# An mLSTM output norm's inverse root: from ScalarE's square root and VectorE's reciprocal to one power on POOL

## The reference, cut to what matters

```python
h = num / jnp.maximum(jnp.abs(den), jnp.exp(-m_t))[..., None]
...
def rmsnorm(x, g):
    xf = x.astype(jnp.float32)
    y = xf * lax.rsqrt(jnp.mean(xf * xf, axis=-1, keepdims=True) + EPS)
    return (y * g).astype(x.dtype)
...
hm = rmsnorm(hm, mlstm_norm_g).astype(x.dtype)
y_b = jax.nn.sigmoid(o) * hm.reshape(B, L, MLSTM_WIDTH)
```

## Time and profile before

| | us |
|---|---|
| median of 3 runs | 1203.65 |
| lowest, highest | 1203.19, 1204.58 |
| the profiled execution, its own time | 1207.14 |
| its span, first to last instruction | 1205.3 |
| TensorE busy in it | 1153.6 |
| VectorE, ScalarE, POOL busy | 704.6, 428.2, 305.3 |

### The profile page before, as it was taken

One profiled execution on the slowest core, in us unless ns is written; L12 is line 12 of the kernel. 1 busy time (PEld: TensorE's weight loads), 2 busy tenths in 40 slices (PEclk: granted clock), 3 DMA queues, 4 the chain that ended last, 5 costly groups with the idle time before them and its releaser, 6 DMA issues.

```text
span 1205.3 us, 19527 instructions
## 1 busy us (share of the span) xinstructions
PE 1153.6 (96%) x7381; PEld 1104.5 (92%) x7381; DVE 704.6 (58%) x1253; ACT 428.2 (36%) x716; POOL 305.3 (25%) x263
## 2 busy tenths in 40 slices
PE   4899999989989999999999999999999999999997
PEld 1698888888978999899999999999999999999996
DVE  5561355577875434777755655655655745656646
ACT  5552354545445343641331320421411311412431
POOL 0441101110525267762120120210210210210352
PEclk9699999999988999999999999999999999999998
DMA  8813434656333822111120121121120211111104
GB/s 307 305 62 110 106 108 137 209 173 197 115 107 106 264 71 72 52 54 36 51 72 23 49 70 36 38 68 34 52 70 17 66 56 32 55 52 36 35 1 141
DMA packets 61702, 109.87 MB, mean 91 GB/s; under 512 B 6434, under 2 KB 30278, under 8 KB 61254
## 3 DMA queue, kind: packets, MB, share of 16 engines
q1 hardware_dynamic: 51430, 84.88, 21.7%
q10 hardware_dynamic: 10208, 24.12, 6.4%
HBM read 96.81 MB, written 12.18 MB: 90 GB/s over the span
## 4 chain that ended last, share of the span: by engine, by line
PE 65%; DVE 2%; ACT 2%; issue 1%; POOL 1%; POOLq 0%; ACTq 0%; DVEq 0%
PE D L2296 13%; PE D L2298 13%; PE D L2297 13%; PE X L2298 5%; PE X L2296 5%; PE X L2297 5%; PE D L2112 3%; PE D L2114 3%; PE D L2113 3%; POOL H_lo L975 0%; DVE X L1556 0%; DVE B L1542 0%; DVE FU L1871 0%; ACT Y_hi L1268 0%; DVE FU L1684 0%
## 5 line engine op out<-in xcount | busy, mean ns | idle before, releaser
L975 POOL TENSOR_TENSOR Y_lo<-FU,Y_hi 128x344 fp32r<-128x344 f32 (+2 forms) x120 | 123.2, 1031 | 560.5 <-ACT Y_hi L1115 554.2
L1831 DVE SCALAR_TENSOR_TENSOR X<-D,MOD,X 128x344 f32<-128x344 f32 (+1 forms) x216 | 123.8, 573 | 136.3 <-PE D L2298 113.8
L2296 PE MATMUL D<-Y_hi,W_hi 128*128 128x344 f32 x576 | 185.2, 322 | 0.0
L2298 PE MATMUL D<-Y_hi,W_lo 128*128 128x344 f32 x576 | 184.1, 320 | 0.0
L2297 PE MATMUL D<-Y_lo,W_hi 128*128 128x344 f32 x576 | 184.1, 320 | 0.0
L2112 PE MATMUL D<-H_hi,W_hi 128*128 128x344 f32 x472 | 160.2, 339 | 3.7 <-POOL H_lo L975 3.1
L2113 PE MATMUL D<-H_lo,W_hi 128*128 128x344 f32 x472 | 153.5, 325 | 0.0
L2114 PE MATMUL D<-H_hi,W_lo 128*128 128x344 f32 x472 | 153.2, 325 | 0.0
L2296 PEld LDWEIGHTS D<-Y_hi,W_hi 128*128 128x128 f32 x576 | 108.5, 188 | 1.2 <-issue 0.9
L970 POOL TENSOR_TENSOR W_lo<-RAWW,W_hi 128x1024 fp32r<-128x1024 f32 x25 | 61.6, 2462 | 186.1 <-ACT W_hi L1110 185.7
L2298 PEld LDWEIGHTS D<-Y_hi,W_lo 128*128 128x128 f32 x576 | 108.5, 188 | 0.0
(11 more groups left out here) (358 smaller groups left out, 2670.8 us busy)
## 6 DMA issues: line engine op xcount, KB each, us to landing
RAWW<-in_W SPq DMA_DIRECT2D x76, 512.0 KB, 3.6
RAWW<-in_WADA ACTq DMA_DIRECT2D x28, 512.0 KB, 4.2
RAWW<-in_WADA SPq DMA_DIRECT2D x20, 512.0 KB, 8.0
RAWW<-in_W ACTq DMA_DIRECT2D x18, 512.0 KB, 4.2
X0T<-in_x SPq DMA_DIRECT2D x3, 1376.0 KB, 12.7
out_y<-OUTN SPq DMA_DIRECT2D x24, 172.0 KB
X<-in_x SPq DMA_DIRECT2D x8, 344.0 KB, 4.6
NM<-nm_d SPq DMA_DIRECT2D x8, 256.0 KB, 5.9
```

Source lines behind the costliest of these rows:

```text
L975: nc.gpsimd.tensor_tensor(lo_v, fu_v, hi_v.bitcast(F32), ALU.subtract).then_inc(lo_ready, 1)
L1831: tell(V.scalar_tensor_tensor(out=tile(X, m_x, a, a + w), in0=DB[bank][:, 0:w], scalar=tile(MOD, m_g, 0, 1), in1=tile(X, m_x, a, a + w), o ...
L2296: T.matmul(out, w_h, hi(kt), start=(kt == 0), stop=False)
L2298: one = T.matmul(out, w_l, hi(kt), start=False, stop=(kt == n - 1))
```

## The change

ScalarE's root in `HN:c` goes. VectorE adds 96 times EPS to the sum of squares in an instruction of its own (row 6 to row 4) and then raises `z_ready`. POOL, in its turn for `HN:c`, waits for `z_ready` and raises row 4 to the power in row 7, which VectorE sets to -0.5 once, in chunk 0. In `HM:c` the reciprocal goes, and the product becomes one of three factors, with the constant sqrt(96).

```diff
@@ POOL @@
+                elif k == "HN":
+                    pool.wait_ge(z_ready, s[1] + 1)
+                    nc.gpsimd.tensor_tensor(SM4[:, 5, :], SM4[:, 4, :], SM4[:, 7, :], ALU.pow).then_inc(z_root, 1)
@@ ScalarE @@
-                elif k == "HN":
-                    act.wait_ge(z_ready, s[1] + 1)
-                    nc.scalar.activation(SM4[:, 5, :], SM4[:, 4, :], ACT.Sqrt, bias=EPT[:], scale=1.0 / HD).then_inc(z_root, 1)
@@ VectorE @@
-                    tell(V.tensor_reduce(SM4[:, 4, :], T1[:, :, 0:HD], AX_X, ALU.add), z_ready, c + 1)
+                    link(V.tensor_reduce(SM4[:, 6, :], T1[:, :, 0:HD], AX_X, ALU.add))
+                    if c == 0:
+                        link(V.memset(SM4[:, 7, :], -0.5))
+                    tell(V.tensor_scalar(SM4[:, 4, :], SM4[:, 6, :], HD * EPS, None, ALU.add), z_ready, c + 1)
...
                     dve.wait_ge(z_root, c + 1)
-                    link(V.reciprocal(SM4[:, 6, :], SM4[:, 5, :]))
-                    tell(V.tensor_tensor(HM[c % 4][:], HM[c % 4][:], wide(SM4[:, 6, :], HD), ALU.mult), hm_ready, c + 1)
+                    tell(V.scalar_tensor_tensor(out=HM[c % 4][:], in0=HM[c % 4][:], scalar=math.sqrt(HD), in1=wide(SM4[:, 5, :], HD),
+                                                op0=ALU.mult, op1=ALU.mult), hm_ready, c + 1)
```

More of the change, by code:

```diff
@@ L11 @@
+import math
 from contextlib import ExitStack
```

## The result

The changed kernel takes **1207.23 us** (median of 7 runs, 1204.93 to 1211.15), the kernel before 1203.65 us on the same chip (7 runs); the ratio is 1.0038, with a 95% interval of 1.0022 to 1.0054. By that ratio it is slower by some 4.6 us; the two medians lie 3.6 us apart. The forecast was 2.3 us less than before, 1201.3 us. The median lies just inside the forecast's range (up to 1207.5 us), on the other side of no change.

The account below looks back on a forecast made before the run. TensorE, busy 1153.6 of 1205.3 us, was taken as the bound. ScalarE's gain of 0.8 us, power losses of 0.6 us and a clock gain of 2.1 us made -2.3 us: 1201.3 us, range 1198.0 to 1207.5.

Parts of the forecast that it names:

- The power's price: POOL's 128x4 power was taken at 0.5 us, between 0.21 and 2.40; rival of a dear power, from 0.57 us, chance 0.21.
- the forecast's own sum without the clock: ScalarE's gain of 0.8 us against 0.6 us of losses at the power: -0.2 us in all.
- -2.1 us for the clock: TensorE's low-clock stretch over 335 to 345 us would go, as the 1.15 us idle ahead of it shrinks: -2.1 us.
- The sum 3p - 0.9 - 0.8: Losses in chunks 1, 3 and 4 at POOL's power price p, less ScalarE's gain of 0.8 us; zero at 0.57 us.
- Chunk 3: VectorE at HM would wait for addition, power and handovers: loss of the power's price less 0.3, so 0.2 us.
- chunk 1: Power stands behind W:12's weight tile, partly covered by VectorE's wait for exp: loss of price less 0.5, so none.
- Chunk 4: Power stands behind YD:0's piece on POOL: loss of price less 0.1, 0.4 us, seen in TensorE's idle 0.79 us.
- Chunk 0: Up to 2.1 us of the power's delay would be covered by EX:1's wait for its DMA.
- chunk 2: VectorE waited 1.7 us there, but no TensorE wait hangs on it: nothing lost.
- "Nothing" in chunks 0, 2 and 5 to 7: Power would cost nothing there: chunk 0 covered by a DMA, 2 without TensorE wait, 5 to 7 POOL free or VectorE late.
- ScalarE's 0.8 us: Without root and table loads, the gelu in chunk 6 starts 0.7 us earlier, with a little from chunk 5: gain 0.8 us.
- The first power: Rival: POOL's first power in chunk 0 comes late from a code fetch; 1201.6 to 1203.7 or 1205.1 to 1207.2 us, chance 0.05.

Follow-up runs that it names:

- three of the kernels: Changed kernel with a product in place of POOL's power, 0.9981; with ScalarE's roots kept into an unused row, 1.0045; with a second power in chunks 2, 5 and 6, 1.0055.
- second powers: Changed kernel with an extra POOL power into an unused row: all chunks 1.0100; 0, 2, 5, 6, 7 1.0079; 2, 5, 6 1.0055; 0, 7 1.0055.
- product to two powers: Changed kernel with POOL's power replaced by a product of the same tiles, 1200.43 us; with a second power in every chunk, 1214.57 us.
- second powers in five and in three chunks: Changed kernel with a second power in chunks 0, 2, 5, 6 and 7, 1211.44 us; in chunks 1, 3 and 4, 1213.84 us.
- the later `HM`: Kernel before with VectorE's HM products of chunks 0 to 5, and the reciprocals ahead of them, moved later in the list: 1206.81 us, 1.0036.

## Why the forecast was wrong

- **The power's price** was mis-sized: 0.5 us against 1.02, inside the bounds of 0.21 and 2.40. The value was taken from the nearest small row, which was another operation. By the forecast's own sum without the clock this turns -0.2 us into +1.4 us. It does not turn the forecast as a whole, as -2.1 us for the clock stood beside it: with that term the sum is zero only at p = 3.8 / 3 = 1.27 us. So two steps failed, this one and the clock's. By the runs the ratio crosses 1 near 0.47 us.
- **Where it lands, in idle time.** The sum 3p - 0.9 - 0.8 gives +1.4 us for p = 1.02; measured +1.7 (15.5 less 13.8). Chunk 3 (p - 0.3 = 0.7, measured 0.8) and chunk 1 (0.5, measured 0.4) came as worked out. That the sum came out so near is in part luck. Chunk 4 (0.9, measured 0.7 and 0.9) has the right number, but not, or not only, by the cause given: the loss is there at a price of 0.20 us too, and the addition that was costed as one small instruction took 2.07 us in three of the kernels. Chunk 0 was called covered by the 2.13 us for which `EX:1` waited; but `ADM:17` (tile MOD) stands between `HM:0` and `EX:1` on VectorE, and TensorE waits for that one, 1.1 us in one of the two profiles. Besides, that slack was 1.07 and 0.38 us in the other two profiles of the kernel before. In chunk 2 the old root came 1.46 to 1.66 us late, behind ScalarE's other work, so POOL brought 0.7 us against two of the three profiles, which the forecast had passed over as nothing.
- **"Nothing" in chunks 0, 2 and 5 to 7** was wrong as a rule: the profiles with second powers show the chunks 0, 2 and 5 handing theirs on nearly in full, in some executions, and chunk 6 handing on 0.5 us in two profiles and nothing in a third. Chunk 7 shows no idle time of TensorE behind it; it was not run by itself.
- **ScalarE's 0.8 us** was not contradicted: the gelu of chunk 6 came where it was put, the last idle time fell by 0.2 to 0.5 us, and keeping the roots cost 0.0007, within the intervals.
- **The clock** was the larger miss. The forecast let it answer with a gain of 2.1 us only, because the idle time ahead of 336.78 would fall below 1 us. It stayed at 1.15 us. The stretch at 335 to 345 us did go, but by luck as far as the profiles tell: it was also gone in the third profile of the kernel before, where the fall came later. And 1.1 us of what it gave was lost at once, for without it TensorE waits 3.05 to 3.07 us and not 1.98 us before the pooling product of 349.40, in the changed kernel as in that third profile. New stretches came between 290 and 330 us, where the idle times had grown. Over the range of prices, product to two powers, the time rose by 14.3 us (0.0119 of 1203); idle time gives 18.8 - 14.1 = 4.7 us of it, 2.6 per us of price and so near the forecast's 3, and the clock's part grew by 13.2 us in those two profiles, whose own times differ by 15.9 us. So the slope of the whole is some three times that of the idle time, by one profile at each end. For the change itself the means of the profiles give 1.7 us idle, where -0.2 was forecast, and (9.9 + 13.2) / 2 - (11.6 + 8.3 + 8.3) / 3 = 2.2 us of clock, where -2.1 was; together 3.9 of the 4.6 us measured. The 2.2 us is less than the 3.3 us by which executions of one kernel differ, so its size is not shown. What is shown is that the falls over 290 to 310 us go with the longer idle time there.
- **The first power** was not late: VectorE's wait for it was 1.21 us in chunk 0 and 1.20 us in chunk 3. The 6 us that the Trainium skill ("GPSIMD Engine Reference", section "Instruction dispatch") gives for the first call to a freshly loaded kernel did not show for this operation.

Open: why the clock fell between 290 and 310 us in four of eight profiles with the same idle time just before; why second powers in five and in three chunks cost more apart than together; and why the later `HM` costs the kernel before 4.3 us.

## What to carry to other kernels

An elementwise operation that an engine has not done in the trace has no neighbour: measure it alone, or forecast both outcomes and give neither a size from another operation. Follow a delay through every instruction that is queued behind it, to the first one that TensorE waits for; slack in front of a DMA, seen in one execution, is no fixed cover. A small instruction that moves beside a large one of POOL can take as long as that one: look where it lands before costing it. Where TensorE is bound, price an added idle time at more than itself: from the product to two powers the time here rose by three times what the idle time did. And read the clock from several executions, as the one that a forecast is read from can be 3 us off.

## What the runs showed of the hardware

- POOL's power of two f32 tiles: 0.55, 0.70, 1.02, 1.63 us for 128 x 1, 2, 4, 8; its product of 128x4 0.20 us. ScalarE's root of 128x4 took 0.30 us, with 11 table loads of 1.28 us for eight roots.
- VectorE and POOL held each other up in these traces. A 128x4 instruction on VectorE that takes 0.17 us elsewhere took 2.42 us where POOL's tile of 1024 columns began 0.01 us before it. VectorE's row, then POOL's, in the changed kernel:

```profile
257.94 2.42 DVE L1723 TENSOR_TENSOR SM<-SM,COL 128x4 f32<-128x4 f32 x1
```

```profile
257.93 2.41 POOL L971 TENSOR_TENSOR W_lo<-RAWW,W_hi 128x1024 fp32r<-128x1024 f32 x1 [14.37 <-ACT W_hi L1114]
```

  The other way round, POOL's power of chunk 6 took 1.99 us in both profiles of the changed kernel; in the first it began at 355.42 us, while VectorE's instruction of 128x1024 ran (354.93 to 356.54).

- In the three profiled executions of the kernel before and the two of the changed one the low stretches of the clock lay elsewhere each time, and the clock's part differed by 3.3 us; TensorE's idle time over 230 to 395 us stayed within 0.4 us.
